# Two transformer blocks on one core: SSD's y turned behind the next chunk's states, and the FFN's norm by halves of the tokens

## The reference, cut to what matters

```python
# SSD (a state space scan), 8 heads of 64, state of 128, in float32
y = ssd_scan(xs * dt[..., None], dt * A, bm, cm)     # by chunks of tokens, a state h carried from chunk to chunk
y = y + d_skip[:, None] * xs
y = y.reshape(b, s, 512) * silu(z)
y_ssd = rmsnorm(y, norm_w)                           # over the 512 features of a token
x = x + g_m * (concatenate([y_ssd, y_att], -1) @ w_out)
# FFN
h = rmsnorm(x, norm_ffn_w) * (1 + sc_f) + sh_f       # over 1024 features
x = x + g_f * conv_ffn(h, w_up, ffn_conv_w, w_down)  # h @ w_up (1024 -> 5632), conv over 3 tokens, gate, @ w_down
x = rmsnorm(x, final_norm_w)
```

## Time and profile before

| | us |
|---|---|
| median of 3 runs | 1814.84 (1812.18 to 1818.27) |
| the profiled execution | 1817.8 |
| its span | 1815.8 |
| PE busy in the span | 1730.4 (95%) |
| DVE busy | 695.8 (38%) |
| ACT busy | 329.3 (18%) |
| mean granted PE clock | 0.977 of full speed |

### The profile page before, as it was taken

One profiled execution on the slowest core, in us unless ns is written; L12 is line 12 of the kernel. 1 busy time (PEld: TensorE's weight loads), 2 busy tenths in 40 slices (PEclk: granted clock), 3 DMA queues, 4 the chain that ended last, 5 costly groups with the idle time before them and its releaser, 6 DMA issues.

```text
span 1815.8 us, 18461 instructions
## 1 busy us (share of the span) xinstructions
PE 1730.4 (95%) x7272; PEld 954.6 (53%) x7272; DVE 695.8 (38%) x1576; ACT 329.3 (18%) x681; POOL 18.7 (1%) x39
## 2 busy tenths in 40 slices
PE   7999899979999999989999999999889999999997
PEld 3445444468888854435444454444454554545452
DVE  4332347677777721030498232312331211212123
ACT  1121224221111110010133433210300000000000
POOL 0001000000000000000000000000000000000001
PEclk8999999999999999999899999999989999999999
DMA  9676110011222222232111110222389999999997
GB/s 403 250 283 210 52 53 40 33 46 48 92 92 92 70 113 74 85 127 93 53 47 47 47 47 1 93 93 93 139 323 410 427 429 429 429 428 429 429 427 315
DMA packets 30239, 335.50 MB, mean 185 GB/s; under 512 B 3208, under 2 KB 5784, under 8 KB 10592
## 3 DMA queue, kind: packets, MB, share of 16 engines
q1 hardware_dynamic: 22464, 310.56, 42.4%
q10 hardware_dynamic: 5168, 14.91, 2.1%
q0 software_dynamic: 2544, 9.18, 1.4%
HBM read 319.66 MB, written 18.37 MB: 186 GB/s over the span
## 4 chain that ended last, share of the span: by engine, by line
PE 82%; DVE 7%; DMA 6%; ACT 3%; issue 1%; POOL 0%; DVEq 0%; SPq 0%; ACTq 0%; POOLq 0%
PE bank L1315 15%; PE bank L963 14%; PE bank L606 10%; PE bank L999 8%; PE bank L1324 6%; PE bank L1124 5%; PE bank L1132 3%; PE bank L778 3%; PE bank L1082 2%; DMA arena<-in_w_expert_up 2%; DMA slot<-in_w_expert_up 2%; PE bank L922 2%; PE bank L588 2%; PE bank L768 2%; PE bank L940 2%
## 5 line engine op out<-in xcount | busy, mean ns | idle before, releaser
L1315 PE MATMUL bank<-slot,arena 128*64 128x512 f32 x704 | 234.7, 599 | 5.5 <-DMA upper<-in_w_expert_up 3.8
L1315 PE MATMUL bank<-upper,arena 128*64 128x512 f32 x352 | 156.3, 599 | 1.9 <-DMA arena<-in_w_expert_up 1.9
L999 PE MATMUL bank<-arena,slot 128*128 128x512 f32 x352 | 151.2, 592 | 0.0
L606 PE MATMUL bank<-hT,slot 128*128 128x512 f32 x272 | 126.7, 626 | 9.2 <-DVE hT L1845 6.5
L1324 PE MATMUL bank<-arena 128*128 128x128 f32 x1024 | 122.9, 280 | 8.5 <-DVE arena L2098 8.5
L1324 PEld LDWEIGHTS bank<-arena 128*128 128x128 f32 x1024 | 118.6, 195 | 20.8 <-issue 12.2
L1315 PEld LDWEIGHTS bank<-slot,arena 128*64 128x64 f32 x704 | 73.0, 138 | 106.2 <-issue 101.3
L2131 DVE TENSOR_TENSOR arena<-arena,bank 128x512 f32<-128x512 f32 x16 | 11.0, 687 | 283.8 <-PE bank L1315 283.8
L1124 PE MATMUL bank<-hT,slot 128*128 128x512 f32 x256 | 114.5, 595 | 1.9 <-DVE arena L1945 1.9
L999 PEld LDWEIGHTS bank<-arena,slot 128*128 128x128 f32 x352 | 67.0, 190 | 83.6 <-issue 83.6
L606 PEld LDWEIGHTS bank<-hT,slot 128*128 128x128 f32 x272 | 53.9, 201 | 79.9 <-issue 75.0
(11 more groups left out here) (401 smaller groups left out, 2217.2 us busy)
## 6 DMA issues: line engine op xcount, KB each, us to landing
slot<-in_w_expert_gate SPq DMA_DIRECT2D x17, 2048.0 KB, 24.5
slot<-in_w_expert_down SPq DMA_DIRECT2D x16, 2048.0 KB, 27.8
slot<-in_w_in SPq DMA_DIRECT2D x15, 2048.0 KB, 8.0
slot<-in_w_ada SPq DMA_DIRECT2D x12, 2048.0 KB, 13.4
slot<-in_w_up SPq DMA_DIRECT2D x11, 2048.0 KB, 8.1
slot<-in_w_expert_up SPq DMA_DIRECT2D x11, 2048.0 KB, 23.3
upper<-in_w_expert_up SPq DMA_DIRECT2D x11, 2048.0 KB, 26.9
upper<-in_w_expert_down SPq DMA_DIRECT2D x6, 2048.0 KB, 28.6
```

The source lines that it names most:

```text
L606: ins = pe.matmul(bank[home[g]][:, :], w[:, k, c0:c0 + P], src[:, k, :], start=(k == 0), stop=(k == KD - 1))
L999: ins = pe.matmul(bank[j][:, :], w[:, k, :], actT[:, k, :], start=(k == 0), stop=(k == FT - 1))
L1315: ins = pe.matmul(dst[b * CAP:(b + 1) * CAP, :], lhs(b, k), rhs(b, k), start=(k == 0), stop=(k == n_k - 1))
```

## The change

In SSD, PE's `turn_y(c - 1)` moves from ahead of the chunk's first `fill(4)` to behind `states(c)` and two more filling matmuls; the fills are 4, 2, 4, 6 (14 in the last chunk) instead of 4, 6, 8 (10), the same 56 in all. On DVE `exponents(c + 1)` now stands ahead of `y_turned(c - 1)`.

In the FFN's entry the norm is done by halves of the tokens: mean plus EPS, Sqrt and reciprocal at 128x256, twice, and the scaling and the shift at 128x256, 16 times instead of 8. The second half takes feature tiles 4 to 7 first, which product 2 needs. PE's products 0, 1 and 2 wait tile by tile for their part (`KD + 4 * p`). The four sums of h's quarters are made in the order in which products 4, 5, 6, 3 take them, each waiting for the one before. The other lines only shift the counts that later waits name.

```diff
--- before.py
+++ after.py
@@ -373,6 +373,8 @@
         junk = view(upper, 7168, NT, P)
 
         OVS = 10
+        HALF = (slice(0, T // 2), slice(T // 2, T))
+        HORDER = (range(KD), (4, 5, 6, 7, 0, 1, 2, 3))
         LAST = ((0, 0), (1, 0), (0, 1), (1, 1), (2, 0), (2, 1), (3, 0), (3, 1))
         UPS = (0, 1, 5, 6, 3, 4, 2)
         UP0 = [(u, p) for p in range(3) for u in range(2)] + [(u, p) for u in range(2) for p in (4, 5, 6, 3)]
@@ -896,14 +898,15 @@
                 outputs(0)
                 fill(10)
                 for c in range(1, NT):
-                    turn_y(c - 1)
                     fill(4)
                     if c + 1 < NT:
                         decays(c + 1)
                     states(c)
-                    fill(6)
+                    fill(2)
+                    turn_y(c - 1)
+                    fill(4)
                     outputs(c)
-                    fill(8 if c + 1 < NT else 10)
+                    fill(6 if c + 1 < NT else 14)
                 turn_y(NT - 1)
             if on("att"):
                 pe.wait_ge(*emptied(G_Q + 3))
@@ -977,8 +980,8 @@
                 pe.wait_ge(S["up_s"], 1)
                 for u, p in UP0:
                     if p in (4, 5, 6, 3):
-                        pe.wait_ge(S["h_part"], 2 * KD + 1 + (4, 5, 6, 3).index(p))
-                    summed(*product(0, u, p), u, p, parts=(KD, KD + 4, None)[p] if u == 0 and p < 3 else None)
+                        pe.wait_ge(S["h_part"], 3 * KD + 1 + (4, 5, 6, 3).index(p))
+                    summed(*product(0, u, p), u, p, parts=KD + 4 * p if u == 0 and p < 3 else None)
                 up_slab(1, 1, base[1])
                 with pe.Fori(1, 5) as i:
                     for j in range(2):
@@ -1014,7 +1017,7 @@
             if on("proj2"):
                 come("qa")
                 for c in range(4):
-                    feature(G_QA + c, slot(0, KD, 512), c * P, parts=2 * KD + 4 if c == 0 else None)
+                    feature(G_QA + c, slot(0, KD, 512), c * P, parts=3 * KD + 4 if c == 0 else None)
                 come("kv")
                 feature(G_KA, slot(1, KD, 256), 0)
                 free(G_VA)
@@ -1658,10 +1661,10 @@
                     own("mt_rdy")
                     if c + 1 < NT:
                         inputs(c + 1)
+                    if c + 1 < NT:
+                        exponents(c + 1)
                     if c >= 1:
                         y_turned(c - 1)
-                    if c + 1 < NT:
-                        exponents(c + 1)
                     seq(ve.tensor_tensor(heads(y2), heads(xstok[:, c, :]), blast(row("d_skip"), HD), ALU.mult))
                     ve.wait_ge(S["y_full"], c + 1)
                     if c == 0:
@@ -1734,24 +1737,26 @@
             if on("ffn"):
                 own("dve_free")
                 seq(ve.scalar_tensor_tensor(aff[:, :], mod[:, 32:40], 1.0, col("norm_ffn", 0, 8), ALU.add, ALU.mult))
-                norm_var(1)
-                ve.wait_ge(S["nroot"], 2)
-                seq(ve.reciprocal(rs, rs))
-                for k in range(KD):
-                    tell(ve.scalar_tensor_tensor(hT[:, k, :], xT[:, k, :], aff[:, k:k + 1], rs, ALU.mult, ALU.mult), "h_raw")
+                ve.wait_ge(S["nsum"], 2)
+                for t in HALF:
+                    tell(ve.tensor_scalar(rs[:, t], bank[6][:, t], 1.0 / D, EPS, ALU.mult, ALU.add), "nvar")
+                for n, t in enumerate(HALF):
+                    ve.wait_ge(S["nroot"], 2 + n)
+                    seq(ve.reciprocal(rs[:, t], rs[:, t]))
+                    for k in HORDER[n]:
+                        tell(ve.scalar_tensor_tensor(hT[:, k, t], xT[:, k, t], aff[:, k:k + 1], rs[:, t], ALU.mult, ALU.mult),
+                             "h_raw")
 
                 def scal(name, i):
                     return cols[:, ds(i + COLS[name][0], 1)] if not isinstance(i, int) else col(name, i)
 
 
-                ve.wait_ge(S["h_part"], 2 * KD)
-                h01, t2, t3, t4 = h_quarter(0, 1), Tq[:, 0:4, :], Tq[:, 4:8, :], Tq[:, 8:12, :]
-                seq(ve.tensor_tensor(t3, h_quarter(1, 1), h01, ALU.subtract))
-                ve.tensor_tensor(h01, h01, h_quarter(0, 0), ALU.subtract).then_inc(S["h_part"], 1)
-                ve.wait_ge(S["h_part"], 2 * KD + 1)
-                ve.tensor_tensor(t2, h_quarter(1, 1), h01, ALU.subtract).then_inc(S["h_part"], 2)
-                ve.wait_ge(S["h_part"], 2 * KD + 3)
-                ve.tensor_tensor(t4, h_quarter(1, 0), t2, ALU.subtract).then_inc(S["h_part"], 1)
+                ve.wait_ge(S["h_part"], 3 * KD)
+                h00, h01, h10, h11 = (h_quarter(k, t) for k in range(2) for t in range(2))
+                t2, t3, t4 = Tq[:, 0:4, :], Tq[:, 4:8, :], Tq[:, 8:12, :]
+                for n, (to, a_, b_) in enumerate(((h01, h01, h00), (t2, h11, h01), (t3, t2, h00), (t4, h10, t2))):
+                    ve.tensor_tensor(to, a_, b_, ALU.subtract).then_inc(S["h_part"], 1)
+                    ve.wait_ge(S["h_part"], 3 * KD + 1 + n)
 
                 def slab(n, j, after, nth):
 
@@ -1839,7 +1844,7 @@
                 seq(ve.tensor_scalar(rs, bank[6][:, :], EPS / D, EPS * EPS, ALU.mult, ALU.add))
                 tell(ve.scalar_tensor_tensor(rs, bank[7][:, :], 1.0 / D, rs, ALU.mult, ALU.add), "nvar")
                 tell(ve.tensor_scalar(rs1, bank[6][:, :], 1.0 / D, EPS, ALU.mult, ALU.add), "nvar")
-                ve.wait_ge(S["nroot"], 3)
+                ve.wait_ge(S["nroot"], 4)
                 seq(ve.reciprocal(rs, rs))
                 for k in range(KD):
                     tell(ve.scalar_tensor_tensor(hT[:, k, :], xT[:, k, :], aff[:, k:k + 1], rs, ALU.mult, ALU.mult), "h_part")
@@ -1917,7 +1922,7 @@
                         ve.wait_ge(*emptied(G_QM + f if f < 4 else G_KM + f - 4))
                         conv(mraw, mconv, f, 5, "ml_cw", 8)
                     elif i == 18:
-                        ve.wait_ge(S["nroot"], 4)
+                        ve.wait_ge(S["nroot"], 5)
                         seq(ve.reciprocal(rs1, rs1))
                     elif i == 22:
                         own("conv_rdy")
@@ -2366,12 +2371,14 @@
                 for m in range(KD):
                     ac.wait_ge(*emptied(G_WA + m))
                     act(hT[:, m, :], xT[:, m, :], ACT.Square, "sq_part")
-                ac.wait_ge(S["nvar"], 2)
-                act(rs, rs, ACT.Sqrt, "nroot")
+                for n, t in enumerate(HALF):
+                    ac.wait_ge(S["nvar"], 2 + n)
+                    act(rs[:, t], rs[:, t], ACT.Sqrt, "nroot")
                 ac.wait_ge(S["mod_rdy"], 2)
-                for k in range(KD):
-                    ac.wait_ge(S["h_raw"], k + 1)
-                    act(hT[:, k, :], hT[:, k, :], ACT.Identity, "h_part", bias=mod[:, 24 + k:25 + k])
+                for n, t in enumerate(HALF):
+                    for i, k in enumerate(HORDER[n]):
+                        ac.wait_ge(S["h_raw"], KD * n + i + 1)
+                        act(hT[:, k, t], hT[:, k, t], ACT.Identity, "h_part", bias=mod[:, 24 + k:25 + k])
 
                 def slab(n, j):
 
@@ -2400,9 +2407,9 @@
                     ac.wait_ge(S["dn_free"], n + 1)
                     act(hT[:, n, :], xT[:, n, :], ACT.Square, "sq_part")
                     act(sqw[:, n, :], xT[:, n, :], ACT.Square, "sq_part", scale=col("final_norm", n))
-                ac.wait_ge(S["nvar"], 3)
+                ac.wait_ge(S["nvar"], 4)
                 act(rs, rs, ACT.Sqrt, "nroot")
-                ac.wait_ge(S["nvar"], 4)
+                ac.wait_ge(S["nvar"], 5)
                 act(rs1, rs1, ACT.Sqrt, "nroot")
             if on("proj2"):
                 ac.wait_ge(S["bias2"], 32)
```

## The result

| | before | changed |
|---|---|---|
| median (lowest to highest), us | 1816.2 (1812.18 to 1818.27), 5 runs | 1804.09 (1802.07 to 1808.49), 5 runs |
| the profiled execution | 1817.8 | 1804.24 |
| its span | 1815.8 | 1802.2 |
| mean granted PE clock, profiled run | 0.977 | 0.982 |

The ratio is 0.9937, with a 95% interval of 0.9925 to 0.995: 11.4 us faster, between 9 and 13.6. The forecast was 9.6 and 1805.2. In what follows one execution of e11, which took 2266.15 at a granted clock of 0.748, is left out.

A forecast was written before the change was run, and what follows sets the result against it. The prediction took PE, 82% of the chain of waits, as the bound: idle time or low clock there costs. SSD's 7.2 plus the FFN's 2.4 gave 9.6 us, from 1814.84 to 1805.2, range 1801 to 1810.

The forecast's parts named there:

- SSD's idle time and the low clock behind the first turn: In SSD, three idle times before turns (5.89 us) and the low clock's cost (1.3) go: 7.2 us together.
- What is queued behind the moved turn: In SSD, PE's fill(4) and outputs and DVE's reordered list are not held up by the moved turn: no cost.
- the spare time: In SSD, y is ready ahead of the three moved turns by 3.8, 3.9 and 2.7 us.
- The FFN's entry, 2.4: At the FFN's entry, half-width norm steps let PE start 2.4 us earlier, 1.6 of it from the reciprocal.
- The clock's loss unchanged: Behind the FFN's pause, the low clock costs what it did, 1.4 us; it may cost nothing or twice that.
- (a): Only SSD counts: FFN's half-width steps save little or the clock stays low longer; 6.9 us, 1807.9, chance 0.10.
- (b): In SSD, a late y moves the pause to the turn's new place: gain 5 to 6 us, about 1809.5, chance 0.08.
- (d): In SSD, the moved turn and outputs form a ring repeating lateness: 6 us slower at 9 us lateness, 1821, chance 0.04.
- (c): Clock losses at other pauses come or go, 2.9 us either way: 1808.1 or 1802.3; outside forecast's range, chance 0.08.
- The rule of the Trainium skill: The clock gate's window is free-running, so pauses behind shifted places draw losses anew: 9.6 us, some 3 either side.

The follow-up runs named there:

- e11: Changed kernel, but on DVE y_turned stands ahead of exponents, as in the kernel before: median 1804.64 us, ratio 0.994 to the kernel before.
- e1: Kernel before with the SSD part of the change alone, FFN's entry as before: median 1808.23 us, ratio 0.9957, 7.8 us gained.
- e5: Changed kernel, but the turn stands behind two fills, ahead of decays and states, DVE's y_turned ahead of exponents: median 1809.21 us, ratio 0.9963.
- e6: Changed kernel, but the turn stands directly behind states, without the two fills between: median 1803.29 us, ratio 0.9932.
- e2: Kernel before with the FFN part of the change alone, SSD as before: median 1812.29 us, ratio 0.9986, 2.5 us gained.
- e4: Changed kernel, but the four sums of h's quarters are made in the order of the kernel before: median 1805.12 us, ratio 0.9945.
- e3: The changed kernel once more, unaltered, against the kernel before: median 1805.83 us, ratio 0.9948, 9.4 us gained.
- e7: Changed kernel, but ACT takes root(3) behind Q's second group's eviction and PE's last turn stands ahead of the last four fills: median 1799.65 us, ratio 0.991.
- e8: Changed kernel with four extra matmuls, results unused, in PE's idle time at the FFN's entry: median 1802.93 us, ratio 0.9924.
- e9: Changed kernel with the edits of e7 and e8 together: median 1799.82 us, ratio 0.9903 to the kernel before.
- e10: e9 plus unused matmuls in the pauses ahead of the second slab's sums (six) and the second block's first projection (seven): median 1796.52 us, ratio 0.9888.

## Why the prediction was right

*SSD's idle time and the low clock behind the first turn, 7.2.* Measured 7.7 between the two profiles and 7.8 in the time of e1. The steps held: the three inner pauses went, the last stayed at 2.44. The chain that the argument hung on (eviction, square, tables, root, scaling: 3.49 behind the end of the fills) is what e5 measured, to about 0.1 us at each turn. The half us more than forecast is in hand-overs: where one `fill` follows another there is none (some 0.3 over all fills), and each of three turns took 0.44 instead of 0.50.

*What is queued behind the moved turn.* That DVE's order costs nothing and gives nothing was right (e11); so was the spare time (e6).

*The FFN's entry, 2.4.* The idle time fell by 2.56. By links: the reciprocals took 1.75 and 1.74 for the 1.75 worked out; the mean plus EPS 0.42 (mean of one) where 0.48 was the bound; the tiles 0.48 and 3.25 for eight, so 0.40 apart, as worked out. The four sums began at 372.16, 7.6 behind PE's first product, and were in time by more than 3 us; e4 shows that their order is of no account. In the time of e2 the part is worth 2.5, with an interval that reaches almost to zero. No run separates the halved reciprocal from the halved scaling and shift; that the reciprocal gives 1.6 of it is read from the trace.

*The clock's loss unchanged.* This term was the loose one, and here the forecast was helped by luck. Between the two profiles the loss rose by 0.7 behind the FFN's first pause and fell by 1.7 at the second slab, by 1.4 at the attention's start and by 2.6 in the second block, which the prediction did not count. For the rise the two profiles show what rival (a) named and the sum left out: the stretch of low clock had begun in the pause, and an earlier return met more of it. That this is a rule is not shown: the new entry's 32 records took 8.83 to 9.79 in the other profiles where the pause was not filled, and 9.71 in e1, whose entry is the old one, with 8.53 before. The prediction had taken the loss as unchanged in the mean, with 3 us to either side; the two heaps of e3, 5 to 6 us apart, are a spread of just that width. The gain of 11.4 lies 1.8 above the forecast, while e1 and e2 add up to 10.3 and e3 and e4 gave 9.4 and 10.0. The time of 1805.2 came out closer than the gain because it was counted from the first three executions of the kernel before (1814.84); from the median of five, 1816.2, the same sum gives 1806.6.

*The rivals.* (a), 6.9 in all, lies below the first comparison's interval (9 to 13.6), but within e3's (6.4 to 12.5); its share for the FFN, 0.7 less 1, lies just below e2's interval. (b), a pause moved to the new place, is in no profile of the changed kernel; (d), the ring, would have shown idle time in front of an inner turn or of outputs, and there is none; e5 has idle time there once the turn stands 5.6 us earlier. (c) happened in part, with the sign of a gain: the losses at some pauses went, and in the medians this came to at most 1.8 of the 2.9 that it allowed. The rule of the Trainium skill, page "TensorE: Matmul & The Clock Gate", section "What's actually happening", that the gate's window runs free of the kernel, is in keeping with the rows, though no run tests it: one pause of 2.9 us, with the same work on either side, was followed by 16 records in 3.72 us in the changed kernel, e2, e3, e4, e5, e7 and e11, in 5.41 in the kernel before, e8 and e9, and in 6.66 and 6.70 in e1 and e6.

## What to carry to other kernels

Where an in-order engine waits for a result, count the chain to that result from the event that really starts it (here another engine's eviction, queued ahead of the square), and place the waiting instruction that long behind it, with independent work between; a few matmuls of margin cost nothing (e6), and a pause that is left can be removed by taking the result ahead of the eviction (e7). Where a whole-width step stands between two stages and the consumer takes halves, halving the slow instruction (the reciprocal of 3.35 us) takes half of it out of the idle time, of which the clock may take back a part (0.7 of 2.6 here), and the order of later steps that have time to spare doesn't matter. And a pause that can't be taken away may be filled with matmuls that nobody reads, if they end before the data comes: it kept the clock at 1.00 at all three places where it was tried. In the time this showed only when the next two pauses were filled too (e10), not with one alone (e8, e9).

## What was not expected of the hardware

The clock is worth as much as one of the parts. Executions of one and the same kernel ran from 1802.07 to 1808.49 with granted clocks from 0.977 to 0.986. Part of the distance between the quick and the slow executions can be read from two profiles, e3's (1802.67) and e6's (1809.43): of 6.8 us between their spans, 3.0 arise at the second slab (records of 3.72 and 6.70 us), 1.0 behind the FFN's first pause, 1.5 at the attention's start and 2.2 in the first part of the second block, all with a lower granted clock in e6; a little is given back elsewhere. This is one pair, of two kernels that differ only in the place of the turn, and not a test. Whether filling pauses narrows the spread is open: e10's four runs lie within 2.2 us at 0.984 to 0.987, but e7's five, with nothing filled, lie within 1.8. Filling one pause alone didn't show in the time when another of 2.9 us followed (e9 against e7). Why that next pause met a fall in e8 and e9, where the first was filled, and in the kernel before, e1 and e6, but in none of seven other profiles in which the first was left open, is not settled.
